# The down blocks of all experts issued by GpSimd on its own queue, in a two-layer decoder trunk with eight experts

## The chip, the cores and the metric

One core of one Trainium2 chip (a NeuronCore). TensorE (PE) multiplies matrices, VectorE (DVE), ScalarE (ACT) and GpSimd (POOL) do the rest, SyncE (SP) mostly starts DMA transfers. 16 DMA engines move the data between the memory of the chip and the core's own SBUF. The metric is the device time of one execution in microseconds (us), as the median of several runs.

## The reference

Two decoder layers over 256 tokens of width 1024, in float32. Each layer has four parallel token mixers (windowed attention, sparse attention, retention, pooling), cross attention into 256 memory tokens, and a feed-forward part, which is dense in layer 0 and made of experts in layer 1. A final norm ends it. The change concerns the experts:

```python
def swiglu(h, w_gu, w_down):
    g, u = jnp.split(h @ w_gu, 2, axis=-1)
    return (jax.nn.silu(g) * u) @ w_down

def moe_ffn(h, router_w, w_gu, w_down):
    logits = (h @ router_w).astype(jnp.float32)
    top_val, top_idx = lax.top_k(logits, TOP_K)            # TOP_K = 2
    top_w = jax.nn.softmax(top_val, axis=-1)
    gate = jnp.sum(jax.nn.one_hot(top_idx, N_EXPERTS, dtype=jnp.float32) * top_w[..., None], axis=-2)
    out = jnp.zeros_like(h)
    for e in range(N_EXPERTS):                             # 8 experts
        out = out + gate[..., e:e + 1] * swiglu(h, w_gu[e], w_down[e])
    return out
```

For each expert `w_gu` is 1024 x 7168 and `w_down` 3584 x 1024: 44 MB of weights an expert, 352 MB for all eight.

## The kernel before

The first 1000 us or so are layer 0 and the mixers of layer 1; the change doesn't touch them. Then come eight jobs, one for each expert, in an order by how many tokens chose the expert: heavy and light ones alternate (`JOB_ORDER = (0, 4, 1, 5, 2, 6, 3, 7)`). Jobs 0, 2, 4, 6 work on three groups of 32 rows, jobs 1, 3, 5, 7 on two. The tokens of an expert are gathered by a matrix of picks and added back by another. `rows_of_next` gathers the rows of the next job after the second down block; for it VectorE has to make the picks (`picks(j)`), and for these GpSimd copies the columns of the job into `slot_now` (`slots_of_job`, L878).

A job takes its weights in 23 blocks (`plan_job`): 8 of the gate matrix (numbers 0 to 7, called G0 to G7 here), 8 of the up matrix (8 to 15, U0 to U7), 7 of the down matrix (16 to 22, D0 to D6; `D0 = 16` in the code is the number of the first). A gate or up block is 128 rows of 3584 floats, one a partition (1.835 MB), a down block 128 partitions of four rows, 4096 floats (2.097 MB). TensorE takes them in the order of their numbers. It takes the last three up blocks (U5 to U7, `up_blocks_by_half`) together: a first half of the products of each (4/7 of the columns), then a second half of each, after which each counts as used.

The blocks live in a ring of 32768 floats a partition, so eight or nine of them at a time. `plan_ring` writes down for each block the place in the ring and, in `FREED_BY`, the last block that must have been used before it may be loaded. For job 3, as an example: D0 waits for U0, D1 for U1, D2 for U2, D3 for U3, D4 for U4, D5 for U5, D6 for U6, and G0 of job 4 for U7, its G1 for D0. Job 7 has the same pattern. In jobs 1 and 5 D3 waits for U4, D4 for U5, D5 for U6, D6 for U7, and the next G0 for D0. In every job D0 waits for U0 of that job. All of this holds for a load by a wait on one semaphore, `expert_used`, which TensorE counts up once a block:

```python
def load_expert(e, o, j):
    buffer = expert_buffer(j, o)
    ...
        sp.wait_ge(expert_used, expert_done(*FREED_BY[j][o]))
    if JOB[o][0] == "d":
        sp.dma_start(buffer.rearrange("p (k n) -> p k n", n=D), expert_source(e, o)).then_inc(expert_landed[o], 16)
    else:
        sp.dma_start(buffer, expert_source(e, o)).then_inc(expert_landed[o], 16)
```

TensorE waits for `expert_landed[o]` before it takes block o. SyncE starts all transfers of blocks, in the order in which they are used, on its one queue (L686 the down blocks, L688 the others). On TensorE the products of gate and up blocks are at L2689, those of down blocks at L2730 and L2737.

Of the kernel before, what the change touches and what calls it, by code (L numbers as in the profile page):

```python
# [55 lines left out]
ROUTE_IDS = 6  # L56
LIGHT = 4
JOB_ORDER = (0, 4, 1, 5, 2, 6, 3, 7)
# [71 lines left out]
def plan_job():  # L130

    return [(w, k) for w in "gu" for k in range(8)] + [("d", k) for k in range(sum(XW) // (P * ROWS))]


def block_floats(step):

    return 1024 * ROWS if step[0] == "d" else sum(XW)


def plan_ring(job, jobs):  # L140

    offsets, freed_by, before, at = [], [], [], 0
    for j in range(jobs):
        offsets.append([])
        freed_by.append([])
        for o, step in enumerate(job):
            size = block_floats(step)
            lo = at if at + size <= RING else 0
            at = lo + size
            offsets[j].append(lo)  # L150
            freed_by[j].append(max([n for n, a, b in before if a < at and lo < b], default=None))
            before.append(((j, o), lo, at))
    return offsets, freed_by


def plan_spare(job):

    offsets, freed_by = plan_ring(job, 1)
    return offsets[0], [n[1] if n else None for n in freed_by[0]]
# [27 lines left out]
def build(nc, x_in, mem_in, positions, norm_mix, w_in, attn_sink, w_branch, w_out, pool_w, pool_scale,  # L187
          norm_cross, norm_mem, w_xq, w_xkv, w_xo, norm_ffn, dense_w_gu, dense_w_down, router_w,
          moe_w_gu, moe_w_down, norm_final, out):
    DEPTH, D = norm_mix.shape  # L190
# [3 lines left out]
    E, F = moe_w_down.shape[1], moe_w_down.shape[2]  # L194
# [7 lines left out]
    JOB = plan_job()  # L202
    OFFSETS, FREED_BY = plan_ring(JOB, E)
    SPARE_OFFSETS, SPARE_FREED_BY = plan_spare(JOB)
# [11 lines left out]
    with ctx:  # L216
        def sb(name, shape, dt=F32):
            return ctx.enter_context(nc.sbuf_tensor(name, shape, dt))
# [7 lines left out]
        def sem(name):  # L226
            return ctx.enter_context(nc.semaphore(name))
# [123 lines left out]
        route_i = sb("route_i", [P, E + ROUTE_IDS + 1], I32)  # L351
        N_MORE = E + ROUTE_IDS
# [22 lines left out]
        def small(layer, name):  # L375
# [21 lines left out]
        expert_landed = [sem(f"expert_landed{i}") for i in range(len(JOB))]  # L397
        expert_used = sem("expert_used")
# [3 lines left out]
                     for b in range(4)]  # L402
# [34 lines left out]
        rank = Signal(sem("rank"), [f"{t} {s}" for t in range(NT) for s in  # L437
                                    ["causal"] + [f"{w}{i}" for i in range(8) for w in ("top", "take")] + ["left", "mask"]])
# [29 lines left out]
        picks_made = sem("picks_made")  # L468
# [37 lines left out]
        def expert_buffer(j, o):  # L506

            at = OFFSETS[j][o] if isinstance(j, int) and j < E else SPARE_OFFSETS[o]
            return ring[:, at:at + block_floats(JOB[o])]
# [5 lines left out]
        def before_experts(lo, hi):  # L515

            half = SLOTS * 4 * UNIT
            slots = [i for i in range(SLOTS) for a in (0, half) if a + i * 4 * UNIT < hi and lo < a + (i + 1) * 4 * UNIT]
            needs = [number(plus(EXPERTS_BASE, i)) + 1 for i in slots]
            if hi > 2 * half:  # L520
                needs.append(chunk_at(DEPTH - 1, "xq3"))
            if hi > 2 * half + 8 * UNIT:
                needs.append(number(plus(EXPERTS_BASE, SLOTS - 1)) + 1)
            return max(needs)

        def expert_done(j, o):

            return j * len(JOB) + o + 1
# [5 lines left out]
        G0, U0, D0, D1 = 0, 8, 16, 20  # L534
# [61 lines left out]
        def expert_source(e, o):  # L596
            which, at = JOB[o]
            if which == "d":
                rows = P * ROWS
                return moe_w_down[0, bass.ds(e, 1), at * rows:(at + 1) * rows, :].rearrange("a (p k) n -> p (a k) n", k=ROWS)  # L600
            col = "gu".index(which) * F
            return moe_w_gu[0, bass.ds(e, 1), at * P:(at + 1) * P, col:col + F].rearrange("a p n -> p (a n)")
# [61 lines left out]
        def _(sp):  # L664
# [8 lines left out]
            def load_expert(e, o, j):  # L673

                buffer = expert_buffer(j, o)
                if not isinstance(j, int):
                    if SPARE_FREED_BY[o] is None:
                        sp.wait_ge(expert_used, expert_done(j - 1, len(JOB) - 1))
                    else:
                        sp.wait_ge(expert_used, expert_done(j, SPARE_FREED_BY[o]))  # L680
                elif FREED_BY[j][o] is None:
                    sp.wait_ge(block_used, before_experts(OFFSETS[j][o], OFFSETS[j][o] + block_floats(JOB[o])))
# [6 lines that stand above are left out]
# [52 lines left out]

            opening = [o for o in range(len(JOB)) if FREED_BY[0][o] is None]
            opening.sort(key=lambda o: before_experts(OFFSETS[0][o], OFFSETS[0][o] + block_floats(JOB[o])))
            for o in opening + list(range(len(opening), len(JOB))):
                load_expert(0, o, 0)
            sp.wait_ge(routed, 1)
            for j in range(1, E):
                rank = JOB_ORDER[j]
                e = sp.value_load(route_i[0:1, rank:rank + 1], min_val=0, max_val=E - 1)
                for o in range(len(JOB)):  # L750
                    load_expert(e, o, j)

            n_more = sp.value_load(route_i[0:1, N_MORE:N_MORE + 1], min_val=0, max_val=ROUTE_IDS)
            with sp.If(n_more > 0):
                with sp.Fori(0, n_more) as k:
                    e = sp.value_load(route_i[0:1, bass.ds(k + E, 1)], min_val=0, max_val=E - 1)
                    for o in range(len(JOB)):
                        load_expert(e, o, k + E)
            sp.wait_ge(x_scaled, n_more + (E - 1))
            sp.nop()  # L760
# [13 lines left out]
        def _(gp):  # L774
# [66 lines left out]
            for layer in range(DEPTH):  # L841
                for n, name in enumerate(ROPE_CHUNKS):
                    for t in range(NT):
# [3 lines left out]
                        a, b, o = rope1[:, t, :], rope2[:, t, :], roped[:, t, :]  # L847
# [29 lines left out]
            def slots_of_job(j):  # L877
                gp.tensor_copy(slot_now[:, :, :, :], job_slots[:, :, :, bass.ds(j, 2)]).then_inc(slots_chosen, 1)  # L878

            slots_of_job(0)  # L880
            gp.wait_ge(routed, 1)
            n_jobs = gp.value_load(route_i[0:1, N_MORE:N_MORE + 1], min_val=0, max_val=ROUTE_IDS) + E
            with gp.Fori(1, n_jobs) as j:
                gp.wait_ge(picks_made, j)
                slots_of_job(j)

# [2007 lines left out]
```

## Time and profile before

| | |
|---|---|
| median of 3 runs | 1851.25 us (1850.29 to 1851.4) |
| the profiled execution | 1851.2 us, its span 1849.3 us |
| TensorE busy | 1790.4 us, 97% of the span |
| VectorE, ScalarE, GpSimd busy | 823.5, 580.6, 57.9 us |
| granted TensorE clock, mean | 0.997 |
| moved by DMA | 526.83 MB, 285 GB/s over the span |
| gate and up blocks | 128 transfers of 1792 KB, 25.3 us from issue to landing (median) |
| down blocks | 56 transfers of 2048 KB, 26.5 us from issue to landing (median) |

The profile is of one execution. Times inside it are counted from the span's start. An engine's row says how long it was busy and in brackets for how long it stood idle before and what ended that. GB/s is what the DMA engines moved. A transfer has two times: its issue (SPq is SyncE as it starts transfers) and its landing, when its semaphore has counted up.

### The profile page before, as it was taken

The numbers are of one execution on the slowest core, as the hardware profiler recorded it, in microseconds if no ns is written. First come the engines' busy times: TensorE is split into PE (matmuls) and PEld (weight loads), VectorE is DVE, ScalarE is ACT, GpSimd is POOL, SyncE is SP. The second block draws the span as 40 slices with busy tenths as digits, with TensorE's granted clock in tenths as the row PEclk, the third lists the DMA queues.
The fourth block names the chain that finished last, engine by engine and source line by source line (L and its number), as shares of the span: only waits on it lengthen the run. The fifth ranks groups of instructions, "written<-read, shape, count | busy, mean of one in ns | idle before, by whom it ended". The sixth has DMA issues, their size and how long they took to land.

```text
span 1849.3 us, 29397 instructions
## 1 busy us (share of the span) xinstructions
PE 1790.4 (97%) x12856; PEld 1096.4 (59%) x12856; DVE 823.5 (45%) x1132; ACT 580.6 (31%) x788; POOL 57.9 (3%) x160
## 2 busy tenths in 40 slices
PE   8999999999999999999999999999988999799987
PEld 7888788888888888778888333333322333233322
DVE  7877777655555676786773320201012020201003
ACT  6556655554344445664462100000000000000001
POOL 4300000000000021000000000000000000000000
PEclk9999999999999999999999999999999999999999
DMA  8445565455555544466556989999999999999996
GB/s 292 155 158 160 160 184 182 158 165 197 185 183 193 182 160 160 157 161 184 182 199 252 377 353 426 426 426 426 426 426 426 426 426 426 427 426 427 425 426 264
DMA packets 127071, 526.83 MB, mean 285 GB/s; under 512 B 7448, under 2 KB 31584, under 8 KB 103392
## 3 DMA queue, kind: packets, MB, share of 16 engines
q1 hardware_dynamic: 126416, 524.66, 74.3%
q8 instruction: 103, 1.69, 0.4%
q10 hardware_dynamic: 528, 0.29, 0.1%
q14 instruction: 24, 0.20, 0.0%
HBM read 523.88 MB, written 1.05 MB: 284 GB/s over the span
## 4 chain that ended last, share of the span: by engine, by line
PE 86%; DMA 11%; DVE 1%; ACT 0%; issue 0%; SPq 0%; DVEq 0%; ACTq 0%
PE bank L2689 22%; PE bank L2231 14%; PE bank L2233 14%; PE bank L2232 14%; DMA ring<-in_moe_w_gu 10%; PE bank L2730 6%; PE bank L2623 3%; PE bank L2737 3%; PE bank L2279 2%; PE bank L2621 2%; DMA ring<-in_moe_w_down 2%; PE bank L2793 1%; PE bank L2297 1%; PE bank L2319 1%; PE bank L2779 0%
## 5 line engine op out<-in xcount | busy, mean ns | idle before, releaser
L2689 PE MATMUL bank<-ring,o_buf 128*32 128x512 f32 (+1 forms) x5120 | 492.7, 543 | 27.4 <-DMA ring<-in_moe_w_gu 27.4
L2231 PE MATMUL bank<-w_hi,stat 128*128 128x512 f32 (+1 forms) x1168 | 458.2, 392 | 0.4 <-DVE low_in_place L2166 0.4
L2233 PE MATMUL bank<-w_hi,stat 128*128 128x512 f32 (+1 forms) x1168 | 453.2, 388 | 0.0
L2232 PE MATMUL bank<-low_in_place,stat 128*128 128x512 f32 (+1 forms) x1168 | 453.1, 388 | 0.0
L1372 DVE TENSOR_TENSOR low_in_place<-raw,w_hi 128x2048 fp32r<-128x2048 f32 (+1 forms) x161 | 368.1, 2288 | 134.3 <-ACT w_hi L896 134.0
L2689 PEld LDWEIGHTS bank<-ring,o_buf 128*32 128x32 f32 x5120 | 165.0, 110 | 356.1 <-issue 310.3
L896 ACT ACTIVATE w_hi<-raw 128x2048 fp32r<-128x2048 f32 (+1 forms) x161 | 305.8, 1904 | 215.4 <-DMA raw<-in_dense_w_gu 60.1
L2231 PEld LDWEIGHTS bank<-w_hi,stat 128*128 128x128 f32 x1168 | 219.8, 188 | 50.1 <-issue 6.0
L2233 PEld LDWEIGHTS bank<-w_hi,stat 128*128 128x128 f32 x1168 | 219.7, 188 | 45.1
L2232 PEld LDWEIGHTS bank<-low_in_place,stat 128*128 128x128 f32 x1168 | 219.9, 188 | 42.8
L1936 DVE TENSOR_TENSOR area<-bank,area 128x512 f32<-128x512 f32 (+1 forms) x32 | 30.7, 1000 | 340.3 <-PE bank L2689 339.9
L2730 PE MATMUL bank<-ring,memT 128*32 128x512 f32 x1024 | 117.5, 593 | 4.9 <-DVE memT L1943 4.9
L1264 ACT ACTIVATE area<-bank 128x512 f32<-128x512 f32 (+1 forms) x48 | 21.8, 560 | 259.5 <-PE bank L2689 259.5
L2730 PE MATMUL bank<-ring,rvg 128*32 128x512 f32 x768 | 89.2, 593 | 9.4 <-DMA ring<-in_moe_w_down 9.4
L1282 ACT ACTIVATE gate<-bank 128x512 f32<-128x512 f32 x7 | 4.2, 598 | 298.7 <-PE bank L2779 298.7
L1994 DVE COPY heads_t<-bank 128x512 f32<-128x512 f32 x8 | 5.5, 692 | 174.5 <-PE bank L2737 94.4
L2730 PEld LDWEIGHTS bank<-ring,memT 128*32 128x32 f32 x1024 | 32.0, 110 | 77.6 <-issue 68.5
L2623 PE MATMUL bank<-stat,w_hi 128*128 128x512 f32 x256 | 68.8, 395 | 0.0
L1980 DVE TENSOR_TENSOR x<-x,bank 128x512 f32<-128x512 f32 x28 | 18.0, 684 | 113.7 <-PE bank L2793 113.7
L2730 PEld LDWEIGHTS bank<-ring,rvg 128*32 128x32 f32 x768 | 24.3, 110 | 69.6 <-issue 52.8
L1287 ACT ACTIVATE heads_t<-bank 128x512 f32<-128x512 f32 x8 | 4.8, 597 | 178.2 <-PE bank L2737 100.5
L2623 PEld LDWEIGHTS bank<-stat,w_hi 128*128 128x128 f32 x256 | 44.5, 188 | 6.8
(346 smaller groups left out, 1290.5 us busy)
## 6 DMA issues: line engine op xcount, KB each, us to landing
ring<-in_moe_w_gu SPq DMA_DIRECT2D x128, 1792.0 KB, 25.3
ring<-in_moe_w_down SPq DMA_DIRECT2D x56, 2048.0 KB, 26.5
raw<-in_w_in SPq DMA_DIRECT2D x55, 1024.0 KB, 4.9
raw<-in_dense_w_gu SPq DMA_DIRECT2D x28, 1024.0 KB, 5.2
raw<-in_w_xkv SPq DMA_DIRECT2D x16, 1024.0 KB, 5.3
raw<-in_dense_w_down SPq DMA_DIRECT2D x14, 1024.0 KB, 5.1
raw<-in_w_branch SPq DMA_DIRECT2D x8, 1024.0 KB, 5.0
raw<-in_w_branch SPq DMA_DIRECT2D x16, 512.0 KB, 6.2
```

The lines of the kernel that those rows point to most:

```text
L896: act.activation(w_hi[:, slot(b), :, 0:width], raw[:, slot(b), :, 0:width], ACT.Copy).then_inc(hi_done, 1)
L1372: dve.tensor_tensor(in_place_lo(b)[:, :, 0:width], raw[:, slot(b), :, 0:width], f32_of(w_hi[:, slot(b), :, 0:width]), ALU.subtract).then_i ...
L1936: ins = dve.tensor_tensor(x_hid[g][:, 0:n].rearrange("q (b k i) -> q b k i", **made), up, silu, ALU.mult)
L2231: pe.matmul(dst, x_hi, wh, start=start, stop=False)
L2232: pe.matmul(dst, x_hi, wl, start=False, stop=False)
L2233: return pe.matmul(dst, x_lo, wh, start=False, stop=stop)
L2279: ins = pe.transpose(b[:, i * P:(i + 1) * P], src, ident[:, :])
L2621: ins = pe.matmul(high, wl[:, k, cols], moving[:, 0, k, :], start=False, stop=False)
L2623: ins = pe.matmul(whole, wh[:, k, cols], moving[:, 0:2, k, :], start=(k == 0), stop=(k == KD - 1))
L2689: ins = pe.matmul(dst[rows_of(q), 0:slab(v)], x_t[:, g, k, :], w[:, q, 4 * v:4 * v + slab(v) // P, :], start=(k == 0), stop=(k == KD - 1))
L2730: ins = pe.matmul(down_banks[0][rows_of(2 * h + a), :], hidden[:, a, m0 + n, :], w[:, at:at + 512], start=(opens and n == 0), stop=(ends a ...
L2737: ins = pe.matmul(down_banks[1][rows_of(2 * h + a), :], hidden[:, 2, m0 + n - 1 + a, :], w[:, at:at + 512], start=(opens and n == 1), stop ...
```

## The change

GpSimd issues the down blocks, on its own queue, with the same waits on the ring. SyncE issues the gate and up blocks only. GpSimd's loop over the jobs is written out for the eight experts, with `load_down` behind `slots_of_job` in each; before, it only copied the slots. The part for further jobs, which runs only when an expert has more than 96 tokens, is changed in the same way.

```diff
--- before.py
+++ after.py
@@ -741,20 +741,20 @@
 
             opening = [o for o in range(len(JOB)) if FREED_BY[0][o] is None]
             opening.sort(key=lambda o: before_experts(OFFSETS[0][o], OFFSETS[0][o] + block_floats(JOB[o])))
-            for o in opening + list(range(len(opening), len(JOB))):
+            for o in opening + list(range(len(opening), D0)):
                 load_expert(0, o, 0)
             sp.wait_ge(routed, 1)
             for j in range(1, E):
                 rank = JOB_ORDER[j]
                 e = sp.value_load(route_i[0:1, rank:rank + 1], min_val=0, max_val=E - 1)
-                for o in range(len(JOB)):
+                for o in range(D0):
                     load_expert(e, o, j)
 
             n_more = sp.value_load(route_i[0:1, N_MORE:N_MORE + 1], min_val=0, max_val=ROUTE_IDS)
             with sp.If(n_more > 0):
                 with sp.Fori(0, n_more) as k:
                     e = sp.value_load(route_i[0:1, bass.ds(k + E, 1)], min_val=0, max_val=E - 1)
-                    for o in range(len(JOB)):
+                    for o in range(D0):
                         load_expert(e, o, k + E)
             sp.wait_ge(x_scaled, n_more + (E - 1))
             sp.nop()
@@ -877,12 +877,30 @@
             def slots_of_job(j):
                 gp.tensor_copy(slot_now[:, :, :, :], job_slots[:, :, :, bass.ds(j, 2)]).then_inc(slots_chosen, 1)
 
+            def load_down(e, j):
+                for o in range(D0, len(JOB)):
+                    if isinstance(j, int):
+                        gp.wait_ge(expert_used, expert_done(*FREED_BY[j][o]))
+                    elif SPARE_FREED_BY[o] is None:
+                        gp.wait_ge(expert_used, expert_done(j - 1, len(JOB) - 1))
+                    else:
+                        gp.wait_ge(expert_used, expert_done(j, SPARE_FREED_BY[o]))
+                    gp.dma_start(expert_buffer(j, o).rearrange("p (k n) -> p k n", n=D), expert_source(e, o)).then_inc(expert_landed[o], 16)
+
             slots_of_job(0)
+            load_down(0, 0)
             gp.wait_ge(routed, 1)
-            n_jobs = gp.value_load(route_i[0:1, N_MORE:N_MORE + 1], min_val=0, max_val=ROUTE_IDS) + E
-            with gp.Fori(1, n_jobs) as j:
+            for j in range(1, E):
                 gp.wait_ge(picks_made, j)
                 slots_of_job(j)
+                rank = JOB_ORDER[j]
+                load_down(gp.value_load(route_i[0:1, rank:rank + 1], min_val=0, max_val=E - 1), j)
+            n_jobs = gp.value_load(route_i[0:1, N_MORE:N_MORE + 1], min_val=0, max_val=ROUTE_IDS) + E
+            with gp.If(n_jobs > E):
+                with gp.Fori(E, n_jobs) as j:
+                    gp.wait_ge(picks_made, j)
+                    slots_of_job(j)
+                    load_down(gp.value_load(route_i[0:1, bass.ds(j, 1)], min_val=0, max_val=E - 1), j)
```

## Rows read from the trace of the kernel before

**Rows 1.** Windows at the jobs' borders: length, PE, PEld, DVE, ACT, POOL, clock, DMA share, GB/s.

```profile
1128.20:1213.10 84.90, 80.27 (x808) 26.43 (x800) 15.94 (x24) 5.28 (x11) 0.19 (x1) 1.00 1.01 426
1213.10:1326.40 113.30, 113.27 (x1152) 38.40 (x1156) 14.63 (x23) 4.09 (x9) 0.19 (x1) 1.00 1.01 426
1326.40:1421.10 94.70, 83.31 (x808) 26.11 (x802) 15.98 (x24) 5.28 (x11) 0.19 (x1) 0.98 1.01 427
...
1743.20:1838.10 94.90, 83.16 (x808) 26.21 (x796) 13.26 (x21) 5.41 (x10) 0.00 (x0) 0.98 0.91 386
```

**Rows 2.** The page's lines on DMA packets and queues, whole span.

```profile
DMA packets 127071, 526.83 MB, mean 285 GB/s; under 512 B 7448, under 2 KB 31584, under 8 KB 103392
...
q1 hardware_dynamic: 126416, 524.66, 74.3%
...
q10 hardware_dynamic: 528, 0.29, 0.1%
```

**Rows 3.** Timeline of TensorE in job 3: U3, U4, and from U7 on.

```profile
1365.21 3.21 PE L2689 MATMUL bank<-ring,o_buf 128*32 128x512 f32 x32 [1.08 <-DMA ring<-in_moe_w_gu]
1369.51 3.21 PE L2689 MATMUL bank<-ring,o_buf 128*32 128x512 f32 x32 [1.08 <-DMA ring<-in_moe_w_gu]
...
1382.38 5.79 PE L2689 MATMUL bank<-ring,o_buf 128*32 128x512 f32 x64 [0.72 <-DMA ring<-in_moe_w_gu]
```

**Rows 4.** Transfers into the ring, window 1357 to 1360: D0 of job 3.

```profile
L686 SPq DMA_DIRECT2D ring<-in_moe_w_down x1: 332/332/332, 1357.8 to 1357.8; - x1
...
DMA to landing us min/median/max: 29.5/29.5/29.5
```

**Rows 5.** Instructions on `slot_now`, and the waits for it.

```profile
L878 POOL COPY slot_now<-shapes x8: 191/192/193, 1036.1 to 1653.0; 128x8 f32 x7, 128x8 f32<-128x8 f32 x1
...
  DVE heads_t L1970: 615.5, 7
```

**Rows 6.** Timeline of TensorE in job 1: 12 gate and up blocks, then D blocks, then job 2.

```profile
1144.21 36.29 PE L2689 MATMUL bank<-ring,o_buf 128*32 128x512 f32 x384
1182.06 7.07 PE L2730 MATMUL bank<-ring,memT 128*32 128x512 f32 x64 [1.56 <-DVE memT L1943]
...
1203.84 3.64 PE L2730 MATMUL bank<-ring,rvg 128*32 128x512 f32 x32 [1.09 <-DMA ring<-in_moe_w_down]
1208.74 3.64 PE L2730 MATMUL bank<-ring,rvg 128*32 128x512 f32 x32 [1.25 <-DMA ring<-in_moe_w_down]
1213.13 9.23 PE L2689 MATMUL bank<-ring,o_buf 128*32 128x512 f32 x96 [0.76 <-DMA ring<-in_moe_w_gu]
```

**Rows 7.** Transfers into the ring: D0 of job 1; landing times of window 1000 to 1030.

```profile
L686 SPq DMA_DIRECT2D ring<-in_moe_w_down x1: 333/333/333, 1159.7 to 1159.7; - x1
...
DMA to landing us min/median/max: 18.7/18.7/18.7
...
DMA to landing us min/median/max: 6.7/10.2/19.8
```

**Rows 8.** Timeline of TensorE in job 2: the last 12 gate and up blocks.

```profile
1233.57 54.33 PE L2689 MATMUL bank<-ring,o_buf 128*32 128x512 f32 x576
```

**Rows 9.** Transfers into the ring, window 1256 to 1257: D0 of job 2.

```profile
L686 SPq DMA_DIRECT2D ring<-in_moe_w_down x1: 337/337/337, 1256.5 to 1256.5; - x1
...
DMA to landing us min/median/max: 26.3/26.3/26.3
```

**Rows 10.** Timeline of TensorE in job 7: U7 and behind it, D5, D6.

```profile
1800.14 7.49 PE L2689 MATMUL bank<-ring,o_buf 128*32 128x512 f32 x64 [2.44 <-DMA ring<-in_moe_w_gu]
...
1829.49 3.64 PE L2730 MATMUL bank<-ring,rvg 128*32 128x512 f32 x32 [0.95 <-DMA ring<-in_moe_w_down]
1834.44 3.64 PE L2730 MATMUL bank<-ring,rvg 128*32 128x512 f32 x32 [1.31 <-DMA ring<-in_moe_w_down]
```

**Rows 11.** Transfers into the ring in job 7: issues of D0, and of D5 and D6.

```profile
L686 SPq DMA_DIRECT2D ring<-in_moe_w_down x1: 332/332/332, 1774.6 to 1774.6; - x1
...
L686 SPq DMA_DIRECT2D ring<-in_moe_w_down x2: 333/333/333, 1805.3 to 1806.6; - x2
```

## Prediction

> **What bounds the kernel now.** I read the windows cut at the jobs' borders first. From 1128 us on, TensorE is busy without a gap in the jobs of three row groups (113.3 us each) and has gaps in the jobs of two (84.9, then 94.7 and 94.9 us), while the 16 DMA engines move 426 GB/s in every window but the last [rows 1]. A pair of jobs takes 208 us, and its bytes, 2 x (16 x 1.835 MB + 7 x 2.097 MB) = 88.1 MB, take 206.7 us at 426 GB/s. So the expert stage is bound by the stream of weights; the heavy jobs only use up a store of landed blocks that the light ones then lack. All of this stream goes through one queue, q1, and its blocks wait in line there: D0 of job 3 takes 29.5 us from issue to landing, where a block alone needs 4.3 to 4.9 us [rows 2, 4].
>
> I then read the light jobs on TensorE, in order of time. U1, U2, ... are the up blocks, D0 to D6 the down blocks. In job 3 TensorE waits for the blocks from U2 on; their starts are 4.3 us apart (a block's transfer), and U7's products begin at 1382.38 us [rows 3]. D0 had been issued at 1357.8 us and landed 29.5 us later, at 1387.3; so U7 landed one D (4.92 us) before, at 1382.4, where TensorE indeed starts it [rows 3, 4]. This is the place to look at: when D0 is issued, six up blocks that are needed sooner are still ahead of it in the line.
>
> **The change, part by part.** What is removed: SyncE no longer issues 56 transfers of 0.33 us [rows 4], 18.6 us that lay on no path: between two of them it waits for TensorE to free a buffer. The waits for free buffers are the same counts on the other engine. These counts only grow from block to block of the plan, so SyncE was never held up by a D in front of a G or U that could have gone earlier: no transfer is issued sooner. GpSimd now reads each expert's number itself; no row shows this read, but it stands right behind `slots_of_job(j)`, and D0 of job j can't be issued before U0 of that job is used, nine blocks into it.
>
> On GpSimd, `slots_of_job(j)` now stands behind the last D of job j-1, which is issued when that job's U7 has been used. Before, it ran once the picks were made: GpSimd idled 615.5 us for it in seven waits, and the copy takes 0.19 us [rows 5]. VectorE needs it at the start of job j, after 7 down blocks (31 us in a light job, 1182.06 to 1213.13) [rows 6]. Cost 0; if that cover were gone, `picks` and with it `rows_of_next` would be late. SyncE also goes on to `norm_final` sooner, a transfer that was not waited for.
>
> What remains is the line. D0 to D6 leave q1 for a queue of their own, and the same 16 engines serve both. The trace never shows two loaded queues (the other dynamic queue moved 0.29 MB) [rows 2], so I bound it from both sides. Lower end: engines serve in order of issue, and nothing moves, 0 us. Upper end: each D goes before all up blocks. D0 to D4 can be issued before U7 is used (D5 and D6 wait for U5 and U6, whose halves end together: 1805.3 in job 7 [rows 11]), so U7 would be late by up to 5 x 4.92 = 24.6 us (4 x 4.92 = 19.7 in jobs 1 and 5, where the ring holds D4 back for U5). I take turns in equal measure: the packets of the experts are whole rows, 14,336 and 16,384 bytes (127071 less 103392 = 23,679 packets of 8 KB or more, against 184 x 128 = 23,552 rows) [rows 2], so nothing in q1 binds eight rows into one turn. While one U block passes (4.31 us), a D block passes too (4.92 us): each us of U work that is left when D0 begins costs 1.14 us.
>
> The rule for this in the Trainium skill, "DMA: Bandwidth & Descriptors", section "Queues, rings and completion order", is that each engine goes round the queues that have work, a packet at a time. It speaks against this change: an issuing engine brings no bandwidth of its own. By that rule the sum is the one below; by order of issue it would be 0. No run shown so far has tried it.
>
> Job 1 (light). D0 was issued at 1159.7 and landed at 1178.4 [rows 7], U7 at 1173.5. An idle line starts moving 2.4 us after the issue (6.7 us shortest, less 4.3) [rows 7], so 1173.5 - 1162.1 = 11.4 us of U are left, U7 comes 13.0 us later, at 1186.5. TensorE ended the up blocks at 1180.5 without waiting, and U7's turn (its first half 1.7, then three second halves of 1.3) came at 1174.9 [rows 6]: it waits 11.6 us. The waits behind it (1.09, 1.25, 0.76) [rows 6] vanish, since the D blocks have gained what the U blocks lost. Job 2 starts 11.6 - 3.1 = 8.5 us late.
>
> Job 2 (heavy). D0 was issued at 1256.5 and landed 26.3 later [rows 9], U7 at 1277.9. With D0 issued 8.5 late, 1277.9 - 1267.4 = 10.5 us are left, U7 comes at 1289.9. TensorE gets there after nine blocks of 4.53 and two first halves of 2.6 from 1233.57 [rows 8], at 1279.5 + 8.5 = 1288.0: 1.9 us more. The lag is 10.4.
>
> Job 3. D0 is issued 10.4 later, so 1382.4 - 1370.6 = 11.8 us of U are left, U7 is late by 13.5, less the waits behind it (job 1's 3.1 stand for all light jobs): 10.4. A lag leaves fewer U blocks in the line at D0's issue, so it limits itself. Job 4 adds nothing (at a lag of 10.4 heavy TensorE comes after U7), job 5 gives 22.2 - 10.4 = 11.8 again, so 10.4. Job 6 adds nothing.
>
> Job 7. D0 was issued at 1774.6 [rows 11], U7 started at 1800.14 [rows 10]: 1800.1 - 1777.0 - 10.4 = 12.7 us of U are left, U7 lands 14.5 us late, at 1814.6. From U7 to the end of D6 TensorE took 38.0 us (1800.14 to 1838.1), 2.3 of it in waits for D5 and D6 (0.95 and 1.31) [rows 10]. D6 lands at 1834.4 as before, since 14.5 / 4.92 = 3 of five D blocks have overtaken, the other two and D5, D6 (issued 5.2 us after U7) keep the engines busy. So D6 ends 14.5 - 2.3 = 12.2 us later, and with it the tail.
>
> **Sum.** Profiled execution 1851.2 us (span 1849.3 and 1.9 around it), 0.05 below the median of 1851.25. 1851.2 + 12.2 = 1863.4. GpSimd's own cost per issue is in no row; below 0.2 us (its copy takes 0.19 [rows 5]), above by the block time of 4.9 us. A D that starts later overtakes less, and D0 to D4 are not what TensorE waits for, so it costs little either way: I round up to 1864.
>
> The Trainium skill, "DMA: Bandwidth & Descriptors", section "Latency and other measured facts", gives about 1 us to the first byte for GpSimd's path and 0.6 for SyncE's, which would shift the D blocks by 0.4 us and this sum by less.
>
> **Rivals.**
> 1. *D blocks first.* If GpSimd's queue gets whole blocks in its turn, TensorE waits 19.7 us at U7 in jobs 1 and 5, 24.6 in jobs 3 and 7, after which the line runs empty until the next D is issued. A light job is otherwise 84.9 - 3.1 = 81.8 us, a heavy one 113.3: 1128.2 + 4 x 81.8 + 2 x (19.7 + 24.6) + 3 x 113.3 = 1883.9 for the end of D6 against 1838.1, +45.8, so 1897. For it: a D is one instruction of eight rows per engine. Against it: packets in q1 are single rows. Decides when a D takes clearly more than half.
> 2. *One D at a time, or D blocks starved.* If GpSimd holds a D back until the one before has landed, a D comes every 4.92 + 2.4 = 7.3 us at best, 51 us in a job whose down phase took 31 (light) or 38.5 (heavy, 1287.9 to 1326.4 [rows 1, 8]): 4 x 20 + 3 x 12.5 = 117 us at most, less what D0 to D4 win by going early (10 in each of eight jobs at most): 37 to 117, or 1888 to 1968. Nothing in the trace speaks for it but that GpSimd has issued no transfer.
> 3. *Order of issue holds*, or the mix costs nothing: 1851. For it: total bytes and issue times are unchanged. Against it: two queues need not know of each other.
> 4. *Faster: two lines fill the engines better.* One line gives 426 GB/s in each window, though the engines' share reads 1.01 [rows 1]. To pay back 12.2 us and win 0.2% (3.7), the 706 us of stream from 1128 to 1834 must shrink by 16, to a rate of 436. No window shows over 427. If it did, 1847.
>
> The Trainium skill, "SBUF — State Buffer", section "SBUF: two separate sides", warns that VectorE can lock GpSimd out of writing descriptors. VectorE is busy 16 us of 84.9 to 94.7 [rows 1], in pieces near 1 us; this delays a D by that at most.
>
> **How the numbers follow.** Equal turns 0.52 (own range 1856 to 1875: an error of a block at U7 either way), D first 0.20, held back or starved 0.11, order of issue 0.10, better rate 0.07. A measurement of this kernel can tell about 0.2% (3.7 us). Slower 0.83, same 0.10, faster 0.07. The range goes from 1850, which takes in "nothing moves", to 1900, past rival 1's time; beyond it lies rival 2.
>
> **What would show it.** D blocks in another queue than q1, with issue to landing near twice 4.9 us, not 29.5; a wait at U7 for the gate and up stream of some 10 us in jobs 1, 3, 5, 7, none at D blocks; windows still at 426 GB/s; last D landing near 1834 us and TensorE still with D blocks in hand. D blocks that land one by one 5 us after issue would be rival 1; D blocks that are waited for, rival 2; a changed rate, rival 4. The prediction is wrong if the share of the two queues is far from equal or the issue on GpSimd is slow.

## Result and profile after

The changed kernel takes 1865.53 us (median of 4 runs, 1864.98 to 1866.1), the kernel before beside it 1851.10 us: a ratio of 1.0079 (95% interval 1.0066 to 1.0091), 14.4 us slower. Predicted were 1864 us and "slower". The profiled execution has a span of 1863.4 us, 14.1 more than before.

The page's queue lines of the changed kernel. They answer to [rows 2]:

```profile
q1 hardware_dynamic: 118352, 407.21, 58.9%
q0 software_dynamic: 8064, 117.44, 15.1%
```

The down blocks, 117.44 MB, have moved to a queue q0. The packet counts tell their size: q0 has 8064 packets for 56 x 128 = 7168 rows (and 56 x 16 = 896 that carry no rows), so a row is counted as a packet there too, as it was in q1.

Windows of the changed kernel at its own job borders (columns as in [rows 1]):

```profile
1128.00:1221.60 93.60, 83.91 (x811) 27.14 (x807) 15.16 (x23) 4.68 (x10) 3.90 (x8) 0.93 0.99 417
1221.60:1338.10 116.50, 113.24 (x1152) 37.58 (x1148) 15.28 (x23) 4.68 (x10) 3.91 (x8) 1.00 1.01 426
1338.10:1432.50 94.40, 83.72 (x810) 27.01 (x806) 15.22 (x23) 4.68 (x10) 3.90 (x8) 0.95 1.01 426
...
1545.50:1642.10 96.60, 84.33 (x808) 27.26 (x804) 15.24 (x23) 4.68 (x10) 3.90 (x8) 0.93 0.97 408
...
1757.70:1852.20 94.50, 83.52 (x808) 26.88 (x800) 13.32 (x21) 5.40 (x10) 3.71 (x7) 0.93 0.85 359
```

Job 1, the first light one, takes 93.6 us instead of 84.9, and job 2 116.5 instead of 113.3 [rows 1]; that is where most of the loss arises. Of the later ones job 3 takes as long as before (94.4 against 94.7 us), job 5 0.7 us longer and job 6 2.5: the lag, once there, stays and grows a little. Now TensorE in job 1, and U6 and U7 of job 7:

```profile
1176.08 2.73 PE L2707 MATMUL bank<-ring,o_buf 128*32 128x512 f32 x16 [2.75 <-DMA ring<-in_moe_w_gu]
1185.27 8.47 PE L2707 MATMUL bank<-ring,o_buf 128*32 128x512 f32 x64 [6.46 <-DMA ring<-in_moe_w_gu]
1194.21 7.07 PE L2748 MATMUL bank<-ring,memT 128*32 128x512 f32 x64 [0.47 <-DVE memT L1961]
...
1211.29 10.48 PE L2748 MATMUL bank<-ring,rvg 128*32 128x512 f32 x96
1221.58 9.20 PE L2707 MATMUL bank<-ring,o_buf 128*32 128x512 f32 x96
...
1806.67 3.64 PE L2707 MATMUL bank<-ring,o_buf 128*32 128x512 f32 x16 [3.86 <-DMA ring<-in_moe_w_gu]
1815.86 7.21 PE L2707 MATMUL bank<-ring,o_buf 128*32 128x512 f32 x64 [5.55 <-DMA ring<-in_moe_w_gu]
```

U6 and U7 come 9.19 us apart (1176.08, 1185.27), where a U block's own transfer takes 4.3 [rows 3]: one U and one D, 4.31 + 4.92 = 9.23, pass in that time. TensorE ran through job 1's up blocks without a wait before [rows 6]; now it waits 2.75 and 6.46 us. Behind it D4 to D6 run as one piece of 10.48 us, where there were waits of 1.09 and 1.25 [rows 6]: TensorE comes so late now that each has landed when it is needed. The issues of the D blocks on GpSimd, from its timeline in job 1, D0 to D3 and D4 (the start, the duration, then the wait):

```profile
1160.44 0.54 POOL L888 DMA_DIRECT2D ring<-in_moe_w_down  x1 [69.47 <-PE bank L2707]
1163.38 0.53 POOL L888 DMA_DIRECT2D ring<-in_moe_w_down  x1 [2.40 <-PE bank L2707]
1166.38 0.53 POOL L888 DMA_DIRECT2D ring<-in_moe_w_down  x1 [2.48 <-PE bank L2707]
1172.39 0.53 POOL L888 DMA_DIRECT2D ring<-in_moe_w_down  x1 [5.48 <-PE bank L2707]
1191.95 0.53 POOL L888 DMA_DIRECT2D ring<-in_moe_w_down  x1 [19.03 <-PE bank L2707]
```

D0 is issued 0.7 us later than SyncE did it (1159.7 [rows 7]), at 0.53 us an issue. GpSimd is not late; D0 is early, since it no longer stands behind U4 to U7: it lands 14.9 us after its issue, at 1175.3, and before U6.

How the engines share out their time can be read from the trace's records of single packets, which the views above do not list. The rows of D0 move from 1164.1 to 1173.8 us, which is 9.7 us, about twice the 4.9 of a D block alone. Between 1165 and 1182 us, when both lines are loaded, I joined each packet to the one that starts as it ends: in 88% of the pairs the queue changes, a U row of 0.54 us, then a D row of 0.61. The first row of D0 starts 3.7 us after the issue.

### The profile page after: what moved, and what is told of

Read it like the earlier page. It is cut to its first block, busy times and chain, and to the rows that moved or that the text cites. A ratio compares the mean times of both kernels' runs of the same rounds, so it can differ in the third digit from the quotient of the medians.

```text
span 1863.4 us, 29395 instructions
## 1 busy us (share of the span) xinstructions
PE 1796.9 (96%) x12856; PEld 1098.0 (59%) x12856; DVE 823.8 (44%) x1132; ACT 580.3 (31%) x788; POOL 87.7 (5%) x217
## 3 DMA queue, kind: packets, MB, share of 16 engines
q0 software_dynamic: 8064, 117.44, 15.1%
## 4 chain that ended last, share of the span: by engine, by line
PE 85%; DMA 12%; DVE 1%; issue 0%; ACT 0%; SPq 0%; DVEq 0%; POOLq 0%; ACTq 0%
PE bank L2707 18%; PE bank L2249 14%; PE bank L2251 14%; PE bank L2250 14%; DMA ring<-in_moe_w_gu 11%; PE bank L2748 9%; PE bank L2641 3%; PE bank L2755 3%; PE bank L2297 2%; PE bank L2639 2%; DMA ring<-in_moe_w_down 1%; PE bank L2811 1%; PE bank L2797 1%; PE bank L2315 1%; PE bank L2337 1%
## 5 line engine op out<-in xcount | busy, mean ns | idle before, releaser
L2707 PE MATMUL bank<-ring,o_buf 128*32 128x512 f32 (+1 forms) x5120 | 501.6, 552 | 44.2 <-DMA ring<-in_moe_w_gu 44.2
L2250 PEld LDWEIGHTS bank<-low_in_place,stat 128*128 128x128 f32 x1168 | 220.1, 188 | 42.6
L2748 PE MATMUL bank<-ring,memT 128*32 128x512 f32 x1024 | 117.5, 594 | 4.2 <-DVE memT L1961 4.2
L2748 PE MATMUL bank<-ring,rvg 128*32 128x512 f32 x768 | 87.7, 593 | 0.9 <-DMA ring<-in_moe_w_down 0.9
L2012 DVE COPY heads_t<-bank 128x512 f32<-128x512 f32 x8 | 5.5, 692 | 164.1 <-PE bank L2755 94.4
L2748 PEld LDWEIGHTS bank<-ring,memT 128*32 128x32 f32 x1024 | 32.1, 110 | 76.8 <-issue 68.5
L888 POOL DMA_DIRECT2D ring<-in_moe_w_down x56 | 29.9, 533 | 755.4 <-PE bank L2707 755.4
L2748 PEld LDWEIGHTS bank<-ring,rvg 128*32 128x32 f32 x768 | 24.9, 110 | 58.6 <-issue 56.5
## 6 DMA issues: line engine op xcount, KB each, us to landing
ring<-in_moe_w_gu SPq DMA_DIRECT2D x128, 1792.0 KB, 17.3
ring<-in_moe_w_down POOLq DMA_DIRECT2D x56, 2048.0 KB, 19.3
```

Source lines behind the costliest of these rows:

```text
L2250: pe.matmul(dst, x_hi, wl, start=False, stop=False)
L2707: ins = pe.matmul(dst[rows_of(q), 0:slab(v)], x_t[:, g, k, :], w[:, q, 4 * v:4 * v + slab(v) // P, :], start=(k == 0), stop=(k == KD - 1))
L2748: ins = pe.matmul(down_banks[0][rows_of(2 * h + a), :], hidden[:, a, m0 + n, :], w[:, at:at + 512], start=(opens and n == 0), stop=(ends a ...
```

## Experiments

Each ratio is against the kernel before, run beside it on the same chip. Theory A is that of the prediction: two lines share the 16 engines in turns, so blocks needed later overtake blocks needed sooner. Rivals: B, what costs is GpSimd's way of starting transfers; C, each light job adds its own share of the 14 us.

**ScalarE issues the D blocks.** It has a hardware queue of its own; the loop goes behind its silu of the job, and GpSimd's loads are taken out (not shown).

```diff
+            def load_down(j):
+                e = act.value_load(route_i[0:1, JOB_ORDER[j]:JOB_ORDER[j] + 1], ...) if j else 0
+                for o in range(D0, len(JOB)):
+                    act.wait_ge(expert_used, expert_done(*FREED_BY[j][o]))
+                    act.dma_start(expert_buffer(j, o)..., expert_source(e, o)).then_inc(expert_landed[o], 16)
             def expert_job(j, first, last=False):
                 expert_silu(j, first)
+                load_down(j)
```

> ScalarE issues the down blocks on its hardware queue (behind its silu of the job), GpSimd issues none. ScalarE's loop over the jobs is written out and its part for further jobs, which does not run here, is left out. Theory A (two lines share the engines in equal turns, so D blocks overtake U blocks; who issues them does not matter): as with GpSimd, 1863 to 1868, U6 and U7 of the light jobs 9.2 us apart, a wait of 5 to 6 us at U7. Theory B (GpSimd's own way of starting transfers is slow, by what it does for each or by how its transfers run): 1850 to 1853, no such waits.

Measured 1863.49 us, ratio 1.0070 (1.0052 to 1.0087). The page's line of the queue, and U6 and U7 of job 7 on TensorE's timeline:

```profile
q10 hardware_dynamic: 8592, 117.74, 15.1%
```

```profile
1806.89 3.64 PE L2709 MATMUL bank<-ring,o_buf 128*32 128x512 f32 x16 [5.08 <-DMA ring<-in_moe_w_gu]
1816.09 7.11 PE L2709 MATMUL bank<-ring,o_buf 128*32 128x512 f32 x64 [5.56 <-DMA ring<-in_moe_w_gu]
```

9.20 us apart and 5.56 us of waiting, within 0.3 us of where they were with GpSimd. Who issues the D blocks does not matter; that they are in a line of their own does.

**GpSimd issues everything in jobs 1 to 7.**

```diff
-            for j in range(1, E):                      # SyncE
-                ...
-                for o in range(D0):
-                    load_expert(e, o, j)
             def load_down(e, j):                       # GpSimd
-                for o in range(D0, len(JOB)):
+                for o in range(len(JOB)):
```

> GpSimd issues all 23 blocks of jobs 1 to 7 in the order in which they are used, SyncE all of job 0 (landings of GpSimd's blocks are counted on ten semaphores in turn). Theory A: one line again, the order of before, 1850 to 1855 (a little is lost where job 1's first blocks share the engines with job 0's last). Theory B: seven jobs of 23 blocks by the slow way instead of eight of 7, that is 2.9 times the blocks: +14 becomes some +40, 1890.

Measured 1852.37 us, ratio 1.0009 (0.9999 to 1.0019), with 308.29 MB through q0, 2.6 times the bytes. D5 and D6 of job 7 on TensorE's timeline stand within 0.5 us of before [rows 10], and wait as they did:

```profile
1829.92 3.64 PE L2751 MATMUL bank<-ring,rvg 128*32 128x512 f32 x32 [1.14 <-DMA ring<-in_moe_w_down]
1834.78 3.64 PE L2751 MATMUL bank<-ring,rvg 128*32 128x512 f32 x32 [1.23 <-DMA ring<-in_moe_w_down]
```

Theory B falls with these two: GpSimd's queue alone carries the stream at no measurable cost, and a hardware queue in its place loses as much.

**Job 7 alone, and all jobs but job 7.** Which jobs' D blocks GpSimd issues is a tuple; their landings are counted on semaphores of their own.

```diff
+DOWN_BY_POOL = (7,)            # the other kernel: (0, 1, 2, 3, 4, 5, 6)
+            of_sync = lambda j: D0 if j in DOWN_BY_POOL else len(JOB)
-                for o in range(D0):
+                for o in range(of_sync(j)):
                     load_expert(e, o, j)
-                load_down(...)
+                if j in DOWN_BY_POOL:
+                    load_down(...)
```

> GpSimd issues the down blocks of job 7 alone, SyncE all others. Theory A: the line is as full at D0's issue as before (23.1 us of U blocks), so five D blocks overtake, U7 is late by 24.6 us, D6 ends 22 us later: 1871 to 1873, more than with all eight jobs. Theory C (each light job adds its own share of the 14 us): 1854 to 1855. Theory B: 7 of 56 blocks, 1853.

> GpSimd issues the down blocks of jobs 0 to 6, SyncE those of job 7. Theory A: the stream of bytes is not behind, only TensorE is (job 7 starts 14.7 us late, at 1757.7), and in job 7 nothing overtakes, so U7 lands near 1800 to 1803 as before; TensorE, with landed blocks in hand, is at U7 after 46.8 us, at 1804.5, and ends D6 at 1804.5 + 38.0 - 2.3 = 1840 instead of 1838: 1852 to 1856. Theory C: 1862. Theory B: 1864.

Job 7 alone: 1866.61 us, ratio 1.0086 (1.0070 to 1.0103). One job of eight costs as much as all eight do, though less than the 1871 to 1873 us that I expected. All but job 7: 1856.55 us, ratio 1.0031 (1.0020 to 1.0043), half a us above what I expected, so seven of eight jobs cost 5.9 us. Theory C (4 and 11 us) falls on both. The up blocks U3 to U7 of job 7 in the first of them, timeline of TensorE:

```profile
1782.07 3.21 PE L2719 MATMUL bank<-ring,o_buf 128*32 128x512 f32 x32 [1.07 <-DMA ring<-in_moe_w_gu]
1790.02 6.10 PE L2719 MATMUL bank<-ring,o_buf 128*32 128x512 f32 x32 [4.74 <-DMA ring<-in_moe_w_gu]
1799.20 3.61 PE L2719 MATMUL bank<-ring,o_buf 128*32 128x512 f32 x16 [3.09 <-DMA ring<-in_moe_w_gu]
1808.39 3.64 PE L2719 MATMUL bank<-ring,o_buf 128*32 128x512 f32 x16 [5.57 <-DMA ring<-in_moe_w_gu]
1817.53 8.58 PE L2719 MATMUL bank<-ring,o_buf 128*32 128x512 f32 x64 [5.50 <-DMA ring<-in_moe_w_gu]
```

The steps grow from 4.3 to 9.2 us as soon as D blocks run beside them. U7 is 17.4 us late (1800.14 before [rows 10]), not the 24.6 expected. Two reasons show. GpSimd's first transfer after a long rest came late:

```profile
1779.10 1.30 POOL L898 DMA_DIRECT2D ring<-in_moe_w_down  x2 [127.10 <-issue]
```

It waited for nothing that the waits show, and was 4.5 us behind the 1774.6 of before [rows 11]. The packet records have a transfer of 8 KB of the kind "instruction" at 1777.2 us, just before it; whether that is what it stood for isn't shown. And D4 was issued at 1796.8 only, since its buffer waits for U4, itself late by then, and landed behind U7 (28.0 us after its issue), so it did not overtake.

In the other kernel TensorE begins job 7 at 1755.58 us (1743.05 before), takes U7 at 1803.00 and ends D6 at 1842.5: it comes with a lag of 12.5 us and leaves with 4.4, because in this one job nothing overtakes and it has landed blocks in hand. That is what theory A says of the lag: TensorE is behind, the stream is not. Expected was 1840; the rest is a wait of 2.38 us for D5.

**Holding D0 back.** Three kernels hold D0 of each job until U5, U6 or U7 has landed.

```diff
                     if isinstance(j, int):
+                        if o == D0:
+                            gp.wait_ge(expert_landed[D0 - 2], expert_in(j))     # U6; D0 - 3: U5, D0 - 1: U7
                         gp.wait_ge(expert_used, expert_done(*FREED_BY[j][o]))
```

> As the changed kernel, but GpSimd holds D0 of each job back until U6 has landed. Theory A (order and equal turns): when D0 starts to move, 0.6 + 2.4 us after U6's landing, 1.3 us of U7 are left; U7 is late by 1.14 x 1.3 = 1.5 us, less than the waits behind it. The gain of the hold is nearly all of the 14 us: 1850 to 1854. Theory C (a second line costs something in each job, whatever the order): 1863 or more.

> D0 held back until U5 has landed. Theory A: 8.6 - 3.0 = 5.6 us of U blocks are left, U7 is late by 6.4, and as D0 is tied to the stream and not to TensorE, this doesn't shrink with TensorE's lag. End of D6: 6.4 - 2.3 = +4.1, so 1853 to 1857, between the hold at U6 and no hold. Theory C: 1863 or more.

> D0 held back until U7 has landed: no block is overtaken at all, but the engines stand still for 0.6 + 2.4 = 3.0 us in each job, since no block behind U7 is issued yet. If the stream of bytes bounds the stage (theory A), seven such gaps are paid in full: +21, 1869 to 1875. If what costs is only the order in which the blocks land, it is as the hold at U6: 1850 to 1854.

Measured: hold at U5 1863.22 us (1.0067, 1.0053 to 1.0080), at U6 1875.49 (1.0147, 1.0130 to 1.0164), at U7 1892.09 (1.0224, 1.0210 to 1.0238). I had expected some 1855, 1852 and 1872. All three are wrong: the longer D0 is held, the worse; two of the holds are worse than none (1865.5), and the shortest cannot be told from it. The wait at U7 did go away with the hold at U6, but TensorE's timeline at the end of job 1 has new ones, for D3 to D6:

```profile
1197.50 3.64 PE L2750 MATMUL bank<-ring,memT 128*32 128x512 f32 x32 [1.66 <-DMA ring<-in_moe_w_down]
1206.78 5.46 PE L2750 MATMUL bank<-ring,rvg 128*32 128x512 f32 x32 [5.64 <-DMA ring<-in_moe_w_down]
1215.99 5.34 PE L2750 MATMUL bank<-ring,rvg 128*32 128x512 f32 x32 [3.75 <-DMA ring<-in_moe_w_down]
1225.19 6.49 PE L2750 MATMUL bank<-ring,rvg 128*32 128x512 f32 x32 [3.85 <-DMA ring<-in_moe_w_down]
```

The D blocks now come 9.2 us apart. At that time SyncE's line has filled again: D0 and D1, once used, have freed the buffers of the next job's gate blocks, and these share the engines with D3 to D6 and overtake them. So there are two borders. In the changed kernel the D blocks have their head start and the second border costs nothing (0.9 us of waits for D blocks at L2748 in all); take the head start away and the loss moves to the second border and is larger. The hold at U7 adds gaps in the stream: in the window of job 1 where D0 is issued (1174.6), the engines are at 0.37 of their share, that is some 3 us without work, as expected. These gaps come on top of the second border.

```profile
1170.00:1175.00 5.00, 5.00 (x56) 1.62 (x52) 0.00 (x0) 0.00 (x0) 0.38 (x1) 1.00 0.37 155
```

**Three lines.** D blocks in turn by GpSimd and ScalarE: `range(D0, len(JOB), 2)` and `range(D0 + 1, len(JOB), 2)` in the two loops above.

> D0, D2, D4, D6 by GpSimd, D1, D3, D5 by ScalarE's hardware queue, the others by SyncE (ScalarE's part for further jobs, which does not run here, is left out). Theory A, turns by queue: with both D lines loaded a U block gets a third, so U blocks of light jobs come up to 4.3 + 2 x 4.92 = 14.1 us apart instead of 9.2. U7's delay reaches the 19.7 to 24.6 us of the D blocks that the ring lets go before it; lags shift between the jobs, 1862 to 1885 in all. If the engines share by bytes between hardware and software queues, or between all U and all D blocks: 9.2 us apart, 1863 to 1868.

Measured 1902.39 us, ratio 1.0293 (1.0269 to 1.0316), above the 1862 to 1885 that I gave. Two rows of TensorE's timeline, U6 and U7 of job 3:

```profile
1399.37 1.93 PE L2712 MATMUL bank<-ring,o_buf 128*32 128x512 f32 x16 [0.36 <-DMA ring<-in_moe_w_gu]
1413.44 2.79 PE L2712 MATMUL bank<-ring,o_buf 128*32 128x512 f32 x12 [12.15 <-DMA ring<-in_moe_w_gu]
```

14.07 us apart, where 4.3 + 2 x 4.92 = 14.1 were expected: turns go by queue, and not by what is left of the work. The distance alone would be the same if each turn took a whole block. The packet records decide it: between 1165 and 1182 us of this kernel's trace the packets, joined as above, come as a U row, a D row of the one queue, a D row of the other, over and over, and the queue changes in 98% of the pairs. This shows the sharing itself; only the sum over the jobs was too low.

**Both borders held.** As the hold at U6, and SyncE starts the next job's gate blocks when D5 has landed.

```diff
+                        if o == D0:
+                            gp.wait_ge(expert_landed[D0 - 2], expert_in(j))
                 e = sp.value_load(...)
+                sp.wait_ge(expert_landed[len(JOB) - 2], expert_in(j - 1))
                 for o in range(D0):
```

> Two holds: D0 of each job until U6 has landed (as the hold at U6 alone, which took 1875 us because the next job's gate blocks then shared the engines with the D blocks), and on SyncE G0 of the next job until D5 has landed. Still two lines, but at each border only one block is in flight when the other line starts, so hardly anything overtakes. If only the order costs: U7 late by some 1.5 us, D6 by some 2.2, both less than the 3.1 us of waits that lie behind them; and the engines stand still for at most a few tenths at a border: 1850 to 1856. If a second line costs by itself, or each start of a line a gap of some us: 1862 or more.

Measured 1856.60 us, ratio 1.0038 (1.0024 to 1.0052): 5.8 us over before, though there are still two lines, and 18.9 less than with the first hold alone. That is 0.6 above the range that I expected. TensorE waits 15.1 us for D blocks in place of 45.9. U7 of jobs 3 and 7, timeline of TensorE:

```profile
1382.83 7.49 PE L2710 MATMUL bank<-ring,o_buf 128*32 128x512 f32 x64 [2.35 <-DMA ring<-in_moe_w_gu]
...
1801.50 5.79 PE L2710 MATMUL bank<-ring,o_buf 128*32 128x512 f32 x64 [1.32 <-DMA ring<-in_moe_w_gu]
```

They stand at 0.45 and 1.36 us behind before [rows 3, 10]. With the order restored the two-line kernel is nearly back. In the profiled execution, the fastest of the five (span 1852.7 us, 3.4 over before), TensorE's waits from 1128 us on are together only 0.5 us longer than before (43.1 against 42.6), while its busy time over the span is 3.1 us longer (1793.5 against 1790.4) for the same 12856 products. So what remains is for the most part work that runs slower behind the waits, as D6 of job 1 does: 5.34 us where it took 3.64 [rows 6]. No version here beats the kernel before, and none is suggested.

## Why the prediction was right

**The place and the mechanism** were right: the order of landing at the border from U to D. ScalarE in GpSimd's place (+12.9 us) and GpSimd alone (+1.8) show that the second line costs and not the engine. **Equal turns**, the step that the prediction chose between two bounds, is confirmed at 9.19 us with two lines and 14.07 with three, and row by row in the packet records. The rule of the Trainium skill, "DMA: Bandwidth & Descriptors", section "Queues, rings and completion order", that an engine goes round its loaded queues a packet at a time, agrees with these two numbers. So rival 1 (D first), rival 2 (D starved or one at a time) and rival 3 (order of issue) all fall. For rival 4 no job's window of the changed kernel is above 426 GB/s.

**The lag from job to job**, start of each job in the changed kernel less that of before, against the prediction:

| start of | before | after | lag | predicted |
|---|---|---|---|---|
| job 2 | 1213.13 | 1221.58 | 8.5 | 8.5 |
| job 3 | 1326.21 | 1338.11 | 11.9 | 10.4 |
| job 4 | 1421.06 | 1432.49 | 11.4 | 10.4 |
| job 5 | 1534.14 | 1545.54 | 11.4 | 10.4 |
| job 6 | 1629.97 | 1642.10 | 12.1 | 10.4 |
| job 7 | 1743.05 | 1757.71 | 14.7 | 10.4 |
| end of D6 | 1838.08 | 1852.18 | 14.1 | 12.2 |

That the lag limits itself is right, and the two kernels with job 7 apart show it best: with a full line ahead of D0 one job costs 15.9 us in the trace (end of D6 at 1854.0), and a job without overtaking gives 8 of 12.5 us back.

**What was too small, and what too large.** In the heavy jobs I had 1.9 us at U7 of job 2 and nothing later; measured are 3.26 in job 2 and 2.35 in job 6. And a term was missing: while TensorE waits at U6 and U7 its clock falls. A window around U7's wait in job 1 of the changed kernel and one of the work behind it, then the like of the first in the kernel before:

```profile
1174.00:1186.00 12.00, 3.46 (x20) 0.62 (x24) 0.00 (x0) 0.00 (x0) 0.00 (x0) 0.63 1.01 427
1186.00:1194.00 8.00, 7.74 (x64) 2.21 (x56) 4.83 (x6) 0.00 (x0) 1.05 (x2) 0.71 0.89 340
```

```profile
1170.00:1181.00 11.00, 10.50 (x112) 3.38 (x104) 4.10 (x5) 0.00 (x0) 0.00 (x0) 1.00 1.01 429
```

The granted clock is 0.63 and 0.71 there (mixes of the two levels, 1.2 and 2.4 GHz) where it was 1.00, and the 64 matrix products from U7's landing on take 8.47, 7.71, 8.18 and 7.21 us in the four light jobs, where the kernel before needs 5.79 in job 3 [rows 3]: 1.4 to 2.7 us more. In job 7 they took 7.49 us before too [rows 10].

How much that is in all can be read from one window over jobs 1 to 7, the kernel before and then the changed one:

```profile
1128.20:1838.10 709.90, 668.21 (x6664) 219.66 (x6656) 104.94 (x159) 33.51 (x70) 1.15 (x6) 1.00 0.99 421
1128.20:1852.20 724.00, 674.76 (x6664) 221.16 (x6656) 104.80 (x159) 33.51 (x70) 27.12 (x55) 0.96 0.98 413
```

The stretch is 14.1 us longer. For the same 6664 products TensorE is busy 6.6 us longer, at a clock of 0.96 instead of 1.00; it is idle 7.5 us longer (49.2 against 41.7). The prediction had put all of its 12.2 us down to waits. So the waits were priced too high and the slower work at nothing, and that the two errors nearly cancel is luck. Job 1 shows it: its lag of 8.5 us is met to 0.1, but TensorE waits 9.2 us at U6 and U7 and not 11.6, and the products of U6 and the 64 from U7's landing on take some 3.9 us longer. The wait for VectorE behind them is 1.1 us shorter (0.47 against 1.56), and 3.7 us come back by job 2 where 3.1 were expected. One reason for the shorter wait is that D0's first row moves 3.7 us after an issue that is itself 0.7 late, not 2.4 after it, so that less of the U blocks was left.

**What was wrong in the signs to look for.** "Windows still at 426 GB/s" holds for jobs 2 and 3, but jobs 1, 4 and 5 show 417, 420 and 408. Blocks that have overtaken are missing behind U7: when it lands, little is left in flight until D4 to D6 are issued, and TensorE's lag delays the issues behind. So the stream has gaps after all, and the last D block does not land near 1834 but at 1839.9 (17.3 us after its issue). "Issue to landing near twice 4.9 us" is wrong as well: 19.3 us in the median, since the D blocks wait for each other in their own line; only the time in which a block's rows move is near twice 4.9 (9.7 for D0 of job 1). The cover of `slots_of_job` held: `slot_now` is copied at 1195.06 in job 1, 26.5 us before job 2 starts. `norm_final`, issued at 1784.83 now, was waited for by nobody.

## What to carry to other kernels

A stream that bounds a kernel is best kept in one queue in the order of use. A second queue added no bandwidth here (no window shown, of either kernel, is above 429 GB/s); it lets blocks needed later take turns with blocks needed sooner, and what a block then takes is its own transfer plus one of each other loaded queue (4.3, 9.2, 14.1 us here). To price such a change, count the work that is still ahead in the line when the first block of the other queue is issued, and look at every border in both directions: a block that is held back at one can be overtaken at the next.

Where each job repeats the same border, the lag of the engine that consumes the stream isn't added up job by job: what it loses before the last job it can win back there, and the last job decides. Moving one job of eight cost as much as moving all. And a forecast of waits is not complete without the work behind them: here TensorE lost 7.5 us in waits and 6.6 by running slower.

## What the runs showed of the hardware that was not expected

- GpSimd's way of issuing costs nothing here that can be measured: an issue takes 0.53 us against SyncE's 0.33 [rows 4], yet the whole stream of seven jobs through its queue is within 0.2% of SyncE's time.
- How soon a transfer starts depends on what the engines are doing. By the packet records D0's first row moves 3.7 to 3.8 us after its issue in jobs 1 to 7 of the changed kernel, and 3.4 to 3.6 us with ScalarE in GpSimd's place; with D0 held until U7 has landed, so that the other line is empty, it is 1.2 us.
- In one place, the first transfer after 127 us of rest (job 7 alone), GpSimd's issue came 4.5 us late, with nothing among the waits to explain it; in the changed kernel, whose GpSimd issues some every 70 us, no such gap shows. The cause is open.
- With rows of 14 and 16 KB, the turns went row by row, and the shares of two and three loaded queues were equal to within 0.1 us a block, whether the other queue was GpSimd's software queue or ScalarE's hardware queue.
